# Rotary queries and keys produced transposed, lower halves moved behind branch sums, a quarter of the last norm on other engines

## The reference

```python
def _apply_partial_rope(x, cos, sin):            # qa, ka: 8 heads x 2 x 64
    x1, x2 = x[..., :8], x[..., 8:16]
    return jnp.concatenate([x1 * c - x2 * sn, x2 * c + x1 * sn, x[..., 16:]], axis=-1)

# first mixer: the branch sum
merged = (gates[:, :, 0] * (a @ w_br_mla) + gates[:, :, 1] * (b @ w_br_moba)
          + gates[:, :, 2] * (c @ w_br_dil))
return merged @ w_out

# end of the second block, last layer
x = _layernorm(DEEPNORM_ALPHA * x + FFN_RES * _swiglu(x, ...), ln3_g[l], ln3_b[l])
```

## Time and profile before

| | us |
|---|---|
| median of three runs | 2759.65 (2759.63 to 2759.92) |
| the profiled execution | 2758.44 |
| its span in the profile | 2756.6 |
| PE busy | 2742.8 (99%) |
| DVE busy | 1821.8 (66%) |
| ACT busy | 1464.0 (53%) |
| POOL busy | 213.0 (8%) |

### The profile page before, as it was taken

The page is one execution under the profiler, slowest core; times in us unless marked ns, Lnnn a source line. Parts: engine busy times, 40 slices in busy tenths (PEclk is TensorE's granted clock), DMA queues, the critical chain, the costliest instruction groups (busy, mean ns, idle before and its releaser), DMA issues.

```text
span 2756.6 us, 44844 instructions
## 1 busy us (share of the span) xinstructions
PE 2742.8 (99%) x18188; PEld 2453.3 (89%) x18188; DVE 1821.8 (66%) x2892; ACT 1464.0 (53%) x2404; POOL 213.0 (8%) x156
## 2 busy tenths in 40 slices
PE   9999999999999999999999999999999999999998
PEld 8989879989989779989988887899899898878997
DVE  6656765646656866656577878775565678787755
ACT  5445655445455645445456566454444565665542
POOL 0010001010010011010012100110100121001100
PEclk9999999999999999999999999999999999999999
DMA  6544445555544445555545344555555554445553
GB/s 247 198 170 163 151 161 189 194 184 199 199 169 152 149 174 200 199 196 199 199 182 195 142 181 148 212 201 194 192 199 194 197 184 153 162 167 184 213 199 123
DMA packets 75069, 504.10 MB, mean 183 GB/s; under 512 B 8784, under 2 KB 10480, under 8 KB 19184
## 3 DMA queue, kind: packets, MB, share of 16 engines
q1 hardware_dynamic: 74576, 501.06, 50.7%
q10 hardware_dynamic: 288, 0.17, 0.0%
HBM read 500.12 MB, written 1.08 MB: 182 GB/s over the span
## 4 chain that ended last, share of the span: by engine, by line
PE 98%; DVE 1%; DMA 0%; issue 0%; ACT 0%; SPq 0%; DVEq 0%
PE ps L1668 48%; PE ps L1688 43%; PE ps L1709 3%; PE ps L1804 1%; PE ps L1802 1%; PE ps L1829 1%; DVE wlo L2167 1%; PE ps L1831 0%; PE ps L1853 0%; DVE g L2378 0%; DMA raw<-in_w 0%; PE ps L1703 0%; PE ps L1820 0%; PE ps L1821 0%; PE ps L1819 0%
## 5 line engine op out<-in xcount | busy, mean ns | idle before, releaser
L1904 ACT ACTIVATE whi<-raw 128x1024 fp32r<-128x1024 f32 (+3 forms) x938 | 976.5, 1043 | 611.5 <-PE ps L1668 400.4
L2167 DVE TENSOR_TENSOR wlo<-raw,whi 128x1024 fp32r<-128x1024 f32 (+2 forms) x894 | 1080.8, 1216 | 273.7 <-ACT whi L1904 272.6
L1688 PE MATMUL ps<-xT_both,whi 128*128 128x256 f32 x6848 | 856.8, 278 | 0.0
L1688 PEld LDWEIGHTS ps<-xT_both,whi 128*128 128x128 f32 x6848 | 813.0, 188 | 6.8 <-issue 5.3
L1668 PE MATMUL ps<-whi,xT_both 128*128 128x512 f32 (+2 forms) x2176 | 586.7, 390 | 2.2 <-ACT whi L1904 1.8
L1668 PEld LDWEIGHTS ps<-whi,xT_both 128*128 128x128 f32 x2176 | 396.2, 188 | 79.8 <-issue 6.6
L1688 PE MATMUL ps<-xT_both,wlo 128*128 128x256 f32 x3424 | 459.3, 277 | 0.0
L1688 PEld LDWEIGHTS ps<-xT_both,wlo 128*128 128x128 f32 x3424 | 421.2, 188 | 0.0
L1668 PE MATMUL ps<-wlo,xT_both 128*128 128x512 f32 (+2 forms) x1088 | 331.2, 385 | 0.3 <-DVE wlo L2167 0.3
L1668 PEld LDWEIGHTS ps<-wlo,xT_both 128*128 128x128 f32 x1088 | 202.1, 188 | 39.1 <-DVE wlo L2167 1.4
L1668 PE MATMUL ps<-whi,hT_hi 128*128 128x512 f32 x704 | 221.4, 390 | 0.0
(11 more groups left out here) (306 smaller groups left out, 2119.8 us busy)
## 6 DMA issues: line engine op xcount, KB each, us to landing
raw<-in_w SPq DMA_DIRECT2D x435, 1024.0 KB, 4.8
vr<-in_vrows SPq DMA_DIRECT2D x19, 512.0 KB, 5.6
raw<-in_w SPq DMA_DIRECT2D x12, 768.0 KB, 4.3
raw<-in_w SPq DMA_DIRECT2D x10, 896.0 KB, 4.5
sums<-scratch SPq DMA_DIRECT2D x8, 512.0 KB, 4.4
raw<-in_w SPq DMA_DIRECT2D x4, 832.0 KB, 4.4
raw<-in_w SPq DMA_DIRECT2D x4, 576.0 KB, 3.7
raw<-in_w SPq DMA_DIRECT2D x4, 512.0 KB, 7.2
```

The lines of the kernel that those rows point to most:

```text
L1688: made = e.matmul(out, ws[:, o:o + 128], xs[:, kt, :], start=kt == 0 and n == 0 and c % 2 == 0, stop=kt == job.nk - 1 and n == 2, skip_gro ...
L1904: e.activation(out, raw, ACT.Copy).then_inc(*mark("hi", i))
L2167: e.tensor_tensor(out, raw, hi.bitcast(F32), sub).then_inc(*mark("lo", i))
```

## The change

Three edits, and two that go with them.

- The chunks `qa` and `ka` are made in the form `columns`, so queries and keys come out transposed. The columns of the weights are permuted beforehand so that the two rotary parts of a half head start 32 partitions apart. For each bank of two heads ScalarE copies four groups of 32 partitions crosswise to `rot`; VectorE multiplies the bank by a cosine table into `qka`, `rot` by a sine table, and adds. The first bank's steps are listed right after the chunk, the second's one background step later. The transposes, the copies after them and the small tiles `rot_t` are gone; the table grows from 128 x 64 to 128 x 512.
- `take` subtracts `slack` from the lookahead for lower halves: 1 from the third branch on in the first mixer, 2 from the middle of its last product, 1 after it, and 0 once the second half of the sum has been transposed.
- For tile 0, half 0 of the last norm VectorE makes the negated mean; ScalarE adds it to the bank and multiplies by the power, GpSimd multiplies by the gain and adds the shift. SP waits for GpSimd ahead of that store.
- GpSimd's scratch for transfers is halved, which makes room.

```diff
 def place(key):
-    if key[0] in ("qk1", "z", "xbc", "qc", "kc"):
+    if key[0] in ("qk1", "z", "xbc", "qa", "ka", "qc", "kc"):
         return COLUMNS_AT
...
-    sbuf("rope2", [128, 2, 32])
+    sbuf("rope2", [128, 2, 256])
...
     def take(self, key, j=0):
-        for part, upto in ((0, self.u + self.reach), (1, self.u + NHL - 1)):
+        for part, upto in ((0, self.u + self.reach), (1, self.u + NHL - 1 - self.slack)):
...
     def branches(...):
             for n in (0, 1):
                 banks, free = self.two()
+                if key == "br1" and i == len(order) - 1:
+                    self.slack = 1
...
                 def mid(tok):
+                    if key == "br1":
+                        self.slack = 2
                     merge(0, tok)
...
             xt.gen += 1
+            self.slack = 0
             yield
+        self.slack = min(self.slack, 1)
         self.fibers.append(other_half())
...
         def rope_chunk(name, n, base):
-            toks = self.gemm((name, l, n), xt, 8, [[(b, 0, 512)] for b in banks], free)
+            outs = [banks[i // 2][:, 256 * (i % 2):256 * (i % 2) + 256] for i in range(4)]
+            tok = self.gemm_w((name, l, n), xt, 8, outs, free)
             def post():
-                bufs = []
-                for t in (0, 1):
+                for j in (0, 1):
                     buf, b_free = rot.get()
-                    self.do("rope2", name, l, n, t, banks[t], toks[t], buf, b_free)
-                    self.main.put(banks[t], ("vec", "rope2", name, l, n, t))
-                    bufs.append(buf)
-                yield
-                yield
-                for k in (0, 2):
-                    ps, p_free = self.aux.get()
-                    self.do("rope2_turn", name, l, n, k, base + 4 * n + k, bufs, ps, p_free, qka)
-                    self.aux.put(ps, ("copy_a", "qka", l, base + 4 * n + k))
-                    if k == 0:
-                        yield
-                for t in (0, 1):
-                    rot.put(bufs[t], ("tr", "rope2", name, l, n, 2))
+                    hh = base + 4 * n + 2 * j
+                    self.do("rope2", l, hh, banks[j], tok, buf, b_free, qka[:, hh:hh + 2, :])
+                    self.main.put(banks[j], ("vec", "cosine", l, hh))
+                    rot.put(buf, ("vec", "rot", l, hh))
+                    yield
             self.spawn(post())
...
     def store(t, n):
-        sp.wait_ge(*at("xn", 12, t, n))
+        sp.wait_ge(*at(*(("pool", "normed", 12) if aside(12, t, n) else ("xn", 12, t, n))))
...
 # ScalarE
-        e.activation(buf[:, :], bank[:, :], ACT.Copy).then_inc(*mark("copy_a", "rope2", name, l, n, t))
+        for g in range(4):
+            made = e.activation(buf[32 * g:32 * g + 32, :], bank[32 * (g ^ 1):32 * (g ^ 1) + 32, :], ACT.Copy)
+        made.then_inc(*mark("copy_a", "swapped", l, hh))
+    def layernorm(en, t, banks, st, mv, ve, r, lg, tg, lb, tb, neg):
+        if neg is not None:
+            half = halves_of(m["x"][t])[0]
+            act.wait_ge(*at("vec", "negated", en, t))
+            e.activation(half, banks[0][:, :], ACT.Identity, bias=neg).then_inc(*mark("act", "centred", en, t))
+            act.wait_ge(*at("act", "centred", en, t))
+            act.wait_ge(*at("rstd", en, t))
+            e.activation(half, half, ACT.Copy, scale=r).then_inc(*mark("act", "scaled", en, t))
...
 # VectorE
+        if neg is not None:
+            e.tensor_scalar(neg, mv[:, 0:1], -1.0, None, mul).then_inc(*mark("vec", "negated", en, t))
         for n in (0, 1):
+            if aside(en, t, n):
+                continue
...
+    def rope2(l, hh, bank, tok, buf, free, out):
+        dve.wait_ge(*at("copy_a", "swapped", l, hh))
+        dve.wait_ge(*at("rope2"))
+        e.tensor_tensor(out, bank[:, :].rearrange("p (a b) -> p a b", a=2), bc1(m["rope2"][:, 0, :], 2), mul
+                        ).then_inc(*mark("vec", "cosine", l, hh))
+        b3 = buf[:, :].rearrange("p (a b) -> p a b", a=2)
+        e.tensor_tensor(b3, b3, bc1(m["rope2"][:, 1, :], 2), mul).then_inc(*mark("vec", "sine", l, hh))
+        dve.wait_ge(*at("vec", "sine", l, hh))
+        e.tensor_tensor(out, out, b3, add).then_inc(*mark("vec", "rot", l, hh))
...
 # GpSimd
-    def layernorm(en, t, banks, st, mv, ve, r, *_):
+    def layernorm(en, t, banks, st, mv, ve, r, lg, tg, lb, tb, neg):
         root(r, ve, en, t)
+        if neg is not None:
+            half = halves_of(m["x"][t])[0]
+            pool.wait_ge(*at("act", "scaled", en, t))
+            e.tensor_tensor(half, half, halves_of(lg)[0], ALU.mult).then_inc(*mark("pool", "gained", en))
+            pool.wait_ge(*at("pool", "gained", en))
+            e.tensor_tensor(half, half, halves_of(lb)[0], ALU.add).then_inc(*mark("pool", "normed", en))
```

More of the change, by code:

```diff
@@ L691, in f @@
                 self.row_half = lambda *_: None
-            self.do("layernorm", e, t, banks, st[t], self.stat(2), self.stat(1), self.stat(1), lg, tg, lb, tb)
+            self.do("layernorm", e, t, banks, st[t], self.stat(2), self.stat(1), self.stat(1), lg, tg, lb, tb,
+                    self.stat(1) if aside(e, t, 0) else None)
             for i in (ig, ib):
@@ L1547, in upper_of, with aside @@
     return ("xhi", *key)
+def aside(e, t, n):
+    return (e, t, n) == (12, 0, 0)
 def bc(ap, n):
@@ L1765, in mla_turn @@
         made.then_inc(*mark("tr", "mlaT", l, h))
-    def rope2_turn(name, l, n, k, at_, bufs, ps, free, _):
-        for f in free:
-            pe.wait_ge(*at(*f))
-        for t in (0, 1):
-            pe.wait_ge(*at("vec", "rot", name, l, n, t))
-        for j in (0, 1):
-            for t in (0, 1):
-                made = transpose(ps[:, 256 * j + 128 * t:256 * j + 128 * t + 128],
-                                 bufs[t][:, 128 * (k + j):128 * (k + j) + 128])
-        made.then_inc(*mark("tr", "rope2", name, l, n, k))
     def conv_out(l, ct, acc, ps, free):
@@ L2105, in halve_b, with rope2 @@
         made.then_inc(*mark("xhi", *key))
-    def rope2(name, l, n, t, bank, tok, buf, free):
+    def rope2(l, hh, bank, tok, buf, free, _):
         act.wait_ge(*at(*tok))
@@ L2217, in final @@
                                    op0=mul, op1=mul).then_inc(*mark("xn", en, t, n))
-    def layernorm(en, t, banks, st, mv, ve, r, lg, tg, lb, tb):
+    def layernorm(en, t, banks, st, mv, ve, r, lg, tg, lb, tb, neg):
         for n in (0, 1):
@@ L2505, in halve_b @@
         made.then_inc(*mark("xlo", *key))
-    rotated = []
-    def rope2(name, l, n, t, bank, tok, buf, free):
-        p3 = bank[:, :].rearrange("p (h d) -> p h d", h=8)[:, :, 0:16]
-        d3 = buf[:, :].rearrange("p (h d) -> p h d", h=8)
-        a3, b3 = (r[:, :].rearrange("p (h d) -> p h d", h=8) for r in m["rot_t"])
-        dve.wait_ge(*at("copy_a", "rope2", name, l, n, t))
-        dve.wait_ge(*at("rope2"))
-        if rotated:
-            dve.wait_ge(*at(*rotated.pop()))
-        e.tensor_tensor(a3, p3, bc1(m["rope2"][:, t, 0:16], 8), mul)
-        e.tensor_tensor(b3, p3, bc1(m["rope2"][:, t, 16:32], 8), mul).then_inc(*mark("vec", "rope2", name, l, n, t))
-        dve.wait_ge(*at("vec", "rope2", name, l, n, t))
-        e.tensor_tensor(d3[:, :, 0:8], a3[:, :, 0:8], b3[:, :, 8:16], sub)
-        e.tensor_tensor(d3[:, :, 8:16], a3[:, :, 8:16], b3[:, :, 0:8], add).then_inc(*mark("vec", "rot", name, l, n, t))
-        rotated.append(("vec", "rot", name, l, n, t))
+    def rope2(l, hh, bank, tok, buf, free, out):
+        dve.wait_ge(*at("copy_a", "swapped", l, hh))
+        dve.wait_ge(*at("rope2"))
+        e.tensor_tensor(out, bank[:, :].rearrange("p (a b) -> p a b", a=2), bc1(m["rope2"][:, 0, :], 2), mul
[4 more added lines that the diff above has]
+        e.tensor_tensor(out, out, b3, add).then_inc(*mark("vec", "rot", l, hh))
     def diff(l, h, p0, p1, d0, d1, r, nlam):
@@ L2698, in constants, with rotary_order @@
     c1, s1, c2, s2 = np.cos(a1), np.sin(a1), np.cos(a2), np.sin(a2)
-    rope = np.concatenate([c1, c1, s1, s1, c2, c2, s2, s2], axis=1).astype(f)
-    rope = np.ascontiguousarray(rope.reshape(2, 128, 96).transpose(1, 0, 2))
-    return np.eye(128, dtype=f), bias, msk, rope
+    rope = np.zeros((128, 2, 320), f)
+    rope[:, :, 0:64] = np.concatenate([c1, c1, s1, s1], axis=1).reshape(2, 128, 64).transpose(1, 0, 2)
+    rope[:, 0, 64:] = 1.0
+    for first in (0, 64):
+        rope[first:first + 8, 0, 64:] = rope[first + 32:first + 40, 0, 64:] = c2.T
+        rope[first:first + 8, 1, 64:] = -s2.T
+        rope[first + 32:first + 40, 1, 64:] = s2.T
+    return np.eye(128, dtype=f), bias, msk, rope
+def rotary_order():
+    order = np.arange(GP + 3072)
+    head = np.r_[0:8, 16:40, 8:16, 40:64]
+    for first in range(QA, QA + 1024, 64):
+        order[first:first + 64] = first + head
+    for first in range(KA, KA + 1024, 64):
+        order[first:first + 64] = first + head
+    return order
 def kernel(**inputs):
```

21 lines of the change are left out of this document (10 added, 11 removed).

## The result

| | before | after |
|---|---|---|
| median, us (six runs each) | 2759.64 (2758.55 to 2760.27) | 2771.51 (2770.46 to 2772.79) |
| ratio, with its 95% interval | | 1.0041 (1.0031 to 1.0052) |
| span of the profiled execution | 2756.6 | 2769.8 |
| rotary stretch, first layer: first matmul of the first chunk to the end of the values' chunk | 1475.41 to 1540.89: 65.48 | 1473.70 to 1547.09: 73.39 |

The forecast was 2768.6 us, with 2757 to 2776 around it. The change made the kernel slower, by 11.9 us, 3 more than the forecast.

A forecast was written before the change was run, and what follows sets the result against it. TensorE, busy 98% of the span, was the bound, with the slower ring of VectorE, ScalarE and GpSimd deciding the forecast. +11.3 - 2.3 - 0.1 = +8.9 us on 2759.65 gave 2768.6 us, range 2757 to 2776.

The forecast's parts named there:

- The ring of VectorE, ScalarE and GpSimd: Second mixer's rotary chunks: one pass through these engines goes from 14.77 to 16.4 us, against 12.6 for TensorE's chunk.
- 1.2, 3.7 and 4.1 us: First layer's rotary stretch: TensorE's forecast waits for GpSimd's second, third and fourth products of the decay weights.
- VectorE's three operations: Rotation of each half chunk: three 128x512 operations, 0.61 + 0.72 + 0.61 = 1.94 us, twice in a pass.
- The copies: ScalarE's four copies of 32 partitions by 512 for each bank: 2.03 us; without overlap, 0.59 each.
- my 16.4: Forecast microseconds of one pass in the rotary chunks: 3.88 + 7.40 + 1.91 + 0.95 + 2.03 + 0.2.
- The third rival: TensorE's clock falls to 1.2 GHz behind its long waits: +5.4 us for two layers, 2774.0 us; chance 0.09.
- The saved transposes: Rotary chunks: 16 groups of four transposes dropped from TensorE at 0.42 us each, 6.7 us in all.
- part one: Rotated queries and keys made transposed, without transposes on TensorE: net +5.65 us a layer, +11.3 for both.
- The upper bound of my sum, 16.1: Rotary change, both layers: copies without any overlap and VectorE operations at 0.69 us each; range +8.3 to +16.1 us.
- Part two: First mixer, lower halves put behind the branch sums: 2.3 of 2.6 us of TensorE's transpose waits gained; bounds 0 to 2.6.
- the 0.15: First mixer: up to 0.15 us left of TensorE's first wait on the branch sums.
- Part three: Last norm: taking 1.5 us off VectorE gains at most 0.14 us, taken as 0.1.

The follow-up runs named there:

- experiment 4: Changed kernel with VectorE's rotation listed two (first bank) and four (second bank) background steps later and the state product one piece later: 2771.49 us.
- experiment 5: Kernel of experiment 4 with VectorE rotating a chunk's second bank a step earlier, ahead of taking in the state product: 2774.72 us.
- experiment 6: Kernel of experiment 5 with the product of the decay weights made by VectorE in GpSimd's place: 2751.95 us, ratio 0.9975 to the kernel before.
- experiment 3: Changed kernel with idle matmuls on TensorE ahead of the third state product, the first group's scale and the fourth state product: 2770.97 us.
- experiment 8: Kernel before with the slack and last-norm edits, and only the last of the four chunks in the new form: 2755.11 us, ratio 0.9987.

## Why the prediction was right, and where it was off

**The place and the mechanism were right.** The ring of VectorE, ScalarE and GpSimd lasts longer than TensorE's chunk, and the difference comes out as TensorE's waits for the product of the decay weights. Forecast for the first layer: 1.2, 3.7 and 4.1 us, the last in part at the scale. Found: 1.22, 4.06 and, at the scale alone, 1.98. VectorE's three operations were put at 1.94 us; from the start of the cosine product at 1504.05 to VectorE's next operation at 1505.98 it is 1.93. The ring is not the only limit, though. I said that nothing else is in it, and that holds for this order; but experiments 4 to 6 show a second limit just as long right behind it, VectorE held up by GpSimd. A repair by order alone fails on that.

**The copies were mis-sized.** I took 3 x 0.48 + 0.59 = 2.03 us from a pair of whole-bank copies and kept 4 x 0.59 for the range. The trace has 2.40, the upper bound. That is 0.37 of the 0.42 by which a pass is longer than my 16.4; the upper half ahead of the copies, 1.06 us up to them (1517.38 to 1518.44) where I had 0.95, adds 0.1. The first copies and the two passes behind them add up: on the clock of the kernel before (the stretch begins 1.71 earlier) the second product ends 0.3 behind my forecast, the third 0.7, and the fourth at 1540.61 where I had 1539.4, 1.2 behind. The Trainium skill, "VectorE: DVE Perf Modes", the trn2 errata, gave 0.57 each for these copies, an estimate of 2.28 for four; the measured 0.60 lies nearer to it than to my 0.48.

**The third rival came in as a small part.** The clock fell to 0.95 in the stretch. Behind the two longest waits 16 matmuls took 2.93 us at a granted clock of 0.69, and four of 512 columns 2.05 at 0.50, its lower level, against 1.07 elsewhere. The Trainium skill, "TensorE: Matmul & The Clock Gate", Part 1, says that idleness lowers the clock; these rows agree. I priced the fall at 2.7 us a layer; experiment 3 shows about 1 us in the first layer and nothing in the second, where the next wait swallows it. In the first layer it and the wait at the scale bring TensorE to the fourth state product 1.17 us after the product is done. In the second layer TensorE waits 0.43 there, and the stretch loses 6.8 instead of 7.9.

**The saved transposes were over-sized** at 0.42 a group; experiments 6 and 8 give (65.49 - 62.57) / 8 = 0.37 (the stretch of 6 without its wait) and 0.34. It hardly entered the sum, because the ring, not TensorE, set the time up to the fourth product.

Together: forecast +11.3 for part one, found 11.87 + 2.86 = 14.7 by the medians and 7.9 + 6.8 = 14.7 by the two stretches. The late fourth product, nearly all of it the copies, makes 2 x 1.2 of the 3.4 that are missing, TensorE's late arrival in the first layer the other 1.1. The upper bound of my sum, 16.1, held it.

**Part two** was put at 2.3 of 2.6 us. No wait on the transposes is left, so all 2.6 are gained, and the 0.15 that I left standing at the first of them is not there. The lower halves that were put off are made up for: no new wait for one appears.

**Part three** was put at 0.1. From the start of the first half's last matmul to VectorE's next operation it was 0.53 us and is 0.43, at 2760.65 and 2761.08, and now VectorE is the one that waits:

```profile
2761.08 0.70 DVE L2274 SCALAR_TENSOR_TENSOR ps<-ps,x 128x512 f32<-128x512 f32 x1 [1.23 <-PE ps L1672]
2761.33 1.27 POOL L2615 TENSOR_TENSOR x<-x,vr 128x512 f32<-128x512 f32 x1
2764.43 0.55 POOL L2601 TENSOR_TENSOR stat<-stat,phalf 128x1 f32<-128x1 f32 x1 [1.83 <-DVE stat L2222]
```

GpSimd is done at 2762.60, 1.8 us ahead of its last power; I had two.

**What stays open:** why VectorE's lateness in experiment 5 costs as much as it does was read from its waits alone, not tried by a change of ScalarE's order. Which of the two order edits of the opening the gain of experiment 6 needs was not tried, nor by a run of its own why the copies of 32 and 64 partitions don't overlap.

## What to carry to other kernels

When the bound engine shows no waits, look for the ring of the other engines that comes out just ahead of it, and add up one pass of it before moving work there: saving some 3 us a layer on TensorE cost some 15 us in all, because it put 2 us into each pass of such a ring. When a ring is opened, ask what its idle time was hiding; here a GpSimd product lay in VectorE's wait, and as soon as VectorE worked there, each met the other. Moving that product to the engine which it held up (1.75 us of work for some 3 of standing still), together with the new order, turned a loss of 12 us into a gain of 7.

## What the runs showed that I had not expected

- Four ScalarE copies of 32 partitions by 512 take 2.40 us, 0.60 each without overlap, whether they exchange partitions or not; two of 64 take 1.20. Copies of a whole bank one after the other take 0.48 up to the next.
- A VectorE operation with both inputs in SBUF stands still until a GpSimd product that began before it is done: 0.42 us became 3.19, 0.68 became 3.40, 0.69 became 3.88. With one input in PSUM it kept its 0.69.
- The same product of 128 x 1536 takes GpSimd 3.5 us and VectorE 1.75.
- GpSimd was slower beside VectorE too: its power of 128 x 2 (line 2601) took 1.61 us at 1533.41 in the changed kernel, where VectorE had begun a lower half at 1533.25, and 0.70 at 1528.01 in experiment 5. TensorE's scale waits for this power. That VectorE is the reason was not tried apart.
